# A transformer feed-forward: the last third of its columns computed as a pair of blocks with seven products in place of eight

## The reference, cut to what matters

```
h2 = RMSNorm(x)
g  = silu(dwconv3(h2 @ ffn_w_gate) + b)      # depthwise, 3 taps along the tokens
x  = x + (g * (h2 @ ffn_w_up)) @ ffn_w_down
```

## Time and profile before

| | us |
|---|---|
| median of 3 runs (lowest, highest) | 2778.08 (2777.70, 2778.23) |
| the profiled execution's own time | 2778.77 |
| its span, first to last instruction | 2776.6 |
| PE busy | 2725.8 |
| DVE busy | 1725.9 |
| ACT busy | 1233.1 |
| POOL busy | 194.7 |
| mean granted TensorE clock, share of 2.4 GHz | 0.996 |

### The profile page before, as it was taken

The page is one execution under the profiler, slowest core; times in us unless marked ns, Lnnn a source line. Parts: engine busy times, 40 slices in busy tenths (PEclk is TensorE's granted clock), DMA queues, the critical chain, the costliest instruction groups (busy, mean ns, idle before and its releaser), DMA issues.

```text
span 2776.6 us, 34468 instructions
## 1 busy us (share of the span) xinstructions
PE 2725.8 (98%) x13320; PEld 2389.1 (86%) x13320; DVE 1725.9 (62%) x2752; ACT 1233.1 (44%) x1872; POOL 194.7 (7%) x334
## 2 busy tenths in 40 slices
PE   7999999999999999999999999999999999999998
PEld 5677766788888998889998889889899999999998
DVE  3665655688567877577876687784364544545353
ACT  5344463466535447336446354454233333333231
POOL 0100011200110000110001000000000000000000
PEclk9999999999999999999999999999999999999999
DMA  9866768843563443853444744435644333443333
GB/s 306 296 222 225 254 202 334 277 148 108 198 238 130 159 140 108 298 180 117 152 136 143 283 147 133 154 119 178 257 137 163 130 118 113 139 148 127 112 113 101
DMA packets 139202, 488.89 MB, mean 176 GB/s; under 512 B 24768, under 2 KB 37440, under 8 KB 122400
## 3 DMA queue, kind: packets, MB, share of 16 engines
q1 hardware_dynamic: 111904, 383.83, 40.7%
q0 software_dynamic: 27136, 102.86, 10.3%
HBM read 397.78 MB, written 88.84 MB: 175 GB/s over the span
## 4 chain that ended last, share of the span: by engine, by line
PE 88%; DMA 4%; DVE 3%; ACT 2%; issue 1%; SPq 0%; POOL 0%; DVEq 0%; ACTq 0%; POOLq 0%
PE bank L1488 43%; PE bank L1504 20%; PE bank L1460 10%; PE bank L1474 7%; PE bank L1567 2%; PE bank L1588 2%; PE bank L1577 2%; DMA cat_lo<-cat_scratch 1%; DMA wraw<-w_out_t 1%; PE bank L1533 1%; PE bank L1553 1%; DVE weights L1086 0%; DVE cc L1189 0%; ACT weights L784 0%; DMA wraw<-w_in_t 0%
## 5 line engine op out<-in xcount | busy, mean ns | idle before, releaser
L1488 PE MATMUL bank<-hw_hi,weights 128*128 128x430 f32 (+1 forms) x4224 | 1190.9, 360 | 0.0
L1488 PEld LDWEIGHTS bank<-hw_hi,weights 128*128 128x128 f32 x4224 | 794.9, 188 | 52.9 <-issue 22.4
L1488 PE MATMUL bank<-hw_lo,weights 128*128 128x430 f32 (+1 forms) x2112 | 755.8, 358 | 0.0
L1086 DVE TENSOR_TENSOR weights<-wraw,weights 128x1024 fp32r<-128x1024 f32 x418 | 510.0, 1220 | 207.2 <-ACT weights L784 206.9
L1504 PE MATMUL bank<-mid,weights 128*128 128x428 f32 x3168 | 629.3, 359 | 0.0
L1504 PEld LDWEIGHTS bank<-mid,weights 128*128 128x128 f32 x3168 | 595.7, 189 | 38.2 <-issue 12.2
L784 ACT ACTIVATE weights<-wraw 128x1024 fp32r<-128x1024 f32 x418 | 440.9, 1055 | 418.4 <-DMA wraw<-w_down_t 272.4
L1189 DVE SCALAR_TENSOR_TENSOR cc<-win,par,cc 128x512 f32<-128x512 f32 x600 | 414.1, 746 | 0.0
L1488 PEld LDWEIGHTS bank<-hw_lo,weights 128*128 128x128 f32 x2112 | 398.8, 189 | 16.6 <-issue 1.0
L1460 PE MATMUL bank<-h_hi,weights 128*128 128x512 f32 x1120 | 367.9, 401 | 13.1 <-DVE weights L1086 13.0
L1460 PEld LDWEIGHTS bank<-h_hi,weights 128*128 128x128 f32 x1120 | 212.5, 190 | 83.8 <-issue 37.3
(11 more groups left out here) (144 smaller groups left out, 1963.3 us busy)
## 6 DMA issues: line engine op xcount, KB each, us to landing
wraw<-w_ffn_t SPq DMA_DIRECT2D x264, 512.0 KB, 3.4
weights<-weight_scratch SPq DMA_DIRECT2D x88, 1024.0 KB, 6.2
wraw<-w_down_t SPq DMA_DIRECT2D x132, 512.0 KB, 3.5
weight_scratch<-weights POOLq DMA_DIRECT2D x22, 1024.0 KB, 7.8
hw_raw<-h_scratch SPq DMA_DIRECT2D x24, 430.0 KB, 4.7
yb<-x_scratch SPq DMA_DIRECT2D x48, 214.0 KB, 3.6
y_t<-yb POOLq DMA_DIRECT2D x48, 214.0 KB, 3.0
cat_hi<-cat_scratch SPq DMA_DIRECT2D x10, 1024.0 KB, 8.3
```

Of the source, the lines that this page charges most:

```text
L1086: nc.vector.tensor_tensor(wlo[n % RING], wraw[n % RING][:], whi[n % RING].bitcast(F32), ALU.subtract) \
L1488: mm = nc.tensor.matmul(out, l[:, k, :], r[:, k, 1:TC + 1] if s else r[:, k, :], start=(k == 0 and j == 0), stop=(k == KT - 1 and j == 2))
```

## The change

The six windows become four plain ones of `TC` = 438 columns (`PLAIN` = 4) and one pair of blocks of `TP` = 406 columns (`TQ` = 408 with the taps' margin). The plain ones run as before. The pair comes after all slots, as a list of its own, `PROD`.

Gate or up of two hidden tiles and both blocks is a product of 2 x 2 blocks: A (weights) is 2 hidden tiles by 2 halves of the 1024 channels, B (activations) is 2 halves of the channels by 2 column blocks. Winograd's form of Strassen's algorithm makes it of seven products with 512 channels each, of 12 matmuls: four sums of weight parts (S1 to S4), four sums of window parts (T1 to T4), and results that are added up partly in the banks (product 6 goes onto 1, then 7 and 4 onto it; 3 onto 5) and partly by DVE (`pair_add`), with ACT copying intermediate states of the banks to `e_buf` (`copy_product`). Group 2i is gate and group 2i+1 is up of hidden tiles 2i and 2i+1: 22 groups. T4 and S4 have the sign that lets product 4 be accumulated.

Down is done as before in number of matmuls, in six passes (`PASSES`): one over 2 hidden tiles, five over 4; each part of a pass is 24 matmuls on a weight tile of 128 x 512, and each pass ends in 16 additions to `yb2`. The order on PE is, from the second group on: products 1 and 5 of a group, product 4 of the one before, a down pass if one is due, then 6, 2, 3, 7.

A weight tile is now 128 x 512 (`part_high` on ACT, `part_low` on DVE, three products ahead, `LEAD`; five high buffers, `HI_RING`). The sums S1 to S4 are made by POOL (`part_sum`) for every group but the first, whose sums are made by DVE during the last plain half, as are T1 to T4; five of the seven window parts are split there, two (T3, T4) in the first steps of the pair. The first of the three taps goes from DVE to ACT (`pair_tap0`), with the bias in the swish. SP loads the four parts of a group two groups ahead (A22 up to three), as soon as the product that read the buffer is over; y's residual for both blocks comes in two loads. POOL stores the pair's outputs after all its sums.

```diff
-TC = 428
-WINDOWS = 6
+PLAIN, PAIRS = 4, 1
+TP = 406
+TC = 2 * -(-(TOKENS + 1 - 2 * PAIRS * TP) // (2 * PLAIN))
...
+KH = KT // 2
+ROW_PAIRS = FT // 2
+GROUPS = 2 * ROW_PAIRS
+PASSES = [[0]] + [[i, i + 1] for i in range(1, ROW_PAIRS, 2)]
+A_OF = {1: "A11", 2: "A12", 3: "S4", 4: "A22", 5: "S1", 6: "S2", 7: "S3"}
+B_OF = {1: "B11", 2: "B21", 3: "B22", 4: "T4", 5: "T1", 6: "T2", 7: "T3"}
+SUMS_READ = {"A11": 3, "S1": 2, "S2": 4, "A12": 4, "S4": 4, "S3": 3, "A22": 1}
+HI_RING = 5
+LEAD = 3
...
+            PROD += [("P", _q, _g, 1), ("P", _q, _g, 5)]
+            if _g > 0:
+                PROD.append(("P", _q, _g - 1, 4))
+            if _s == 0 and _i > 0 and PASS_OF[_i] != PASS_OF[_i - 1]:
+                PROD += [("D", _q, PASS_OF[_i - 1], _j) for _j in range(down_parts(PASS_OF[_i - 1]))]
+            PROD += [("P", _q, _g, _p) for _p in (6, 2, 3, 7)]
...
+for _gi in range(ALL_GROUPS):
+    _gate = _gi % 2 == 0
+    for _e, _p in enumerate((1, 5, 6)):
+        ACT_AT[at(_gi, _p) + 1].append(("copy", _gi, _e))
+    for _x, _p in enumerate((2, 3, 7, 4)):
+        _t = at(_gi, _p) + 1
+        if _x < 3:
+            DVE_AT[_t].append(("add", _gi, _x))
+        if _gate:
+            ACT_AT[_t].append(("tap0", _gi, _x))
+        else:
+            DVE_AT[_t].append(("product", _gi, _x))
+            ACT_AT[_t].append(("mid_high", _gi, _x))
...
+    _t = max(_t, _k - (1 if PROD[_k][0] == "D" and PROD[_k][3] >= 3 else LEAD))
...
+        ACT_AT[_t].append(("high", _k))
+        DVE_AT[_t].append(("low", _k))
...
+        if _gate:
+            DVE_AT[_t + 1].append(("taps", _gi, _x))
+            ACT_AT[_t + 2].append(("swish", _gi, _x))
+        elif _x == 3 and _t < PRODS and PROD[_t][0] == "D":
+            DVE_AT[_t].append(("mid_low", _gi, _x))
+        else:
+            DVE_AT[_t + 1].append(("mid_low", _gi, _x))
...
+    DVE_AT[_k + 1].append(("y_add", _k))
...
+    for _a, _k in (("A11", at(_gi - 2, 1)), ("A12", at(_gi - 2, 2)), ("A22", at(max(_gi - 3, 0), 4)), ("A21", at(_gi - 2, 7))):
+        SP_AT[max(_k, at(_gi - 2, 1)) + 1].append(("weights", _gi, _a))
...
+            def part_sum(gi, a):
+                n = 4 * gi
+                if gi >= 2 and a != "S3":
+                    pool.wait_ge(s_used, SLOTS + at(gi - 2, {"S1": 5, "S2": 6, "S4": 3}[a]) + 1)
...
+                two = {"S1": ("A21", "A22"), "S2": ("S1", "A11"), "S3": ("A21", "A11"), "S4": ("A12", "S2")}[a]
...
+                nc.gpsimd.tensor_tensor(p_raw[part_key(gi, a)][:], p_raw[part_key(gi, two[0])][:], p_raw[part_key(gi, two[1])][:],
+                                        ALU.add if a == "S1" else ALU.subtract).then_inc(s2_s, 1)
...
+            def part_low(k):
+                t = PROD[k]
+                dve.wait_ge(s_whi, SPLITS[-1] + k + 1)
+                if t[0] == "P":
+                    gi = GROUPS * t[1] + t[2]
+                    dve.wait_ge(s2_s, 4 * gi + SUMS_READ[A_OF[t[3]]])
+                nc.vector.tensor_tensor(p_lo[part_of(k)][:], p_raw[part_of(k)][:], p_hi[k % HI_RING][:].bitcast(F32),
+                                        ALU.subtract).then_inc(s_wlo, 1)
...
+            def pair_product(k, q, g, p):
+                gi = GROUPS * q + g
+                gate = gi % 2 == 0
+                pe.wait_ge(s_wlo, SPLITS[-1] + k + 1)
...
+                if p == 1 and gi >= 2:
+                    pe.wait_ge(s_c3 if gate else s_m, H_PLAIN + 4 * hidden_pair(gi - 2) + 4)
+                elif p == 5 and gi >= 1:
+                    pe.wait_ge(s2_add, 3 * (gi - 1) + 2)
+                elif p == 2 and gi >= 1:
+                    pe.wait_ge(s2_add, 3 * (gi - 1) + 1)
+                elif p == 6:
+                    pe.wait_ge(s2_e, 3 * gi + 1)
+                elif p == 7:
+                    pe.wait_ge(s2_e, 3 * gi + 3)
+                elif p == 3:
+                    pe.wait_ge(s2_e, 3 * gi + 2)
+                elif p == 4:
+                    pe.wait_ge(s2_add, 3 * gi + 3)
...
+                for t in range(KH):
+                    for j, (l, r) in enumerate(((a, hi), (a, lo), (b, hi))):
+                        mm = nc.tensor.matmul(out, l[:, t, :], r[:, t, cols], start=(p in (1, 2, 5) and t == 0 and j == 0),
+                                              stop=(t == KH - 1 and j == 2), skip_group_check=(p in (3, 4, 6, 7)))
...
+            def pair_down(k, q, F, j):
+                pe.wait_ge(s_wlo, SPLITS[-1] + k + 1)
...
+                for n, o, i in y_outputs(k):
+                    if j == 0:
+                        pe.wait_ge(s_mlo, H_PLAIN + 4 * u + (3 if i == 1 else 4))
+                    if n >= 4:
+                        pe.wait_ge(s_y, Y_PLAIN + n - 3)
```

More of the change, by code:

```diff
@@ L72 @@
 PHASES += [("A", CHUNKS - 1, 0, A_HEAD), ("O", 0), ("A", CHUNKS - 1, A_HEAD, PROJ)]
-for _w in range(WINDOWS):
+for _w in range(PLAIN):
     PHASES.append(("F", _w, 0))
@@ L662, in _ @@
                         load_residual(c)
+                if n in PAIR_LOADS:
+                    load_pair_window(0, PAIR_LOADS[n])
+                if n == LAST + GU_TILES:
+                    for a in ("A21", "A22", "A11", "A12"):
+                        load_part(0, a)
+            for a in ("A21", "A22", "A11", "A12"):
+                load_part(1, a)
+            for d in range(3):
+                load_down(d)
+            for k in range(PRODS):
+                for t in SP_AT[k]:
+                    if t[0] == "weights":
+                        load_part(t[1], t[2])
+                    elif t[0] == "down":
+                        load_down(t[1])
+                    elif t[0] == "window":
+                        load_pair_window(t[1], t[2])
+                    elif t[0] == "y":
+                        load_pair_y(t[1], t[2])
         @block.gpsimd
@@ L1080, in _ @@
                         window_high(0, p)
+                if n in PAIR_ACT:
+                    pair_window_high(*PAIR_ACT[n][1:])
+            for k in range(FIRST_SPLITS):
+                part_high(k)
+            for k in range(PRODS + 4):
+                for t in ACT_AT[k]:
+                    if t[0] == "copy":
+                        copy_product(t[1], t[2])
+                    elif t[0] == "tap0":
+                        pair_tap0(t[1], t[2])
+                    elif t[0] == "swish":
+                        pair_swish(t[1], t[2])
+                    elif t[0] == "mid_high":
+                        pair_mid_high(t[1], t[2])
+                    elif t[0] == "high":
+                        part_high(t[1])
+                    elif t[0] == "window_high":
+                        pair_window_high(t[1], t[2])
         @block.vector
@@ L1331, in y_add, with first_part_sum @@
                                         ALU.add).then_inc(s_y, 1)
+            def first_part_sum(a):
+                two = {"S1": ("A21", "A22"), "S2": ("S1", "A11"), "S3": ("A21", "A11"), "S4": ("A12", "S2")}[a]
+                for t in two:
+                    if t in SUM_ORDER:
+                        dve.wait_ge(s2_s, SUM_ORDER.index(t) + 1)
+                    else:
+                        dve.wait_ge(s2_w[t in ("A21", "A22")][0], 32)
+                nc.vector.tensor_tensor(p_raw[part_key(0, a)][:], p_raw[part_key(0, two[0])][:], p_raw[part_key(0, two[1])][:],
+                                        ALU.add if a == "S1" else ALU.subtract).then_inc(s2_s, 1)
@@ L1375, in _ @@
                     norm2_add(before[1], before[2])
[L1376 removed]
+                if now[0] == "D" and now[2] == 1 and now[1] + 1 < PLAIN and 3 <= now[3] < 3 + PIECES:
                     window_low(now[1] + 1, now[3] - 3)
@@ L1411, in _ @@
                         window_low(0, p)
-                conv_ops(*CONV_OPS_AT[n])
+                if n in PAIR_DVE:
+                    t = PAIR_DVE[n]
+                    if t[0] == "window_sum":
+                        pair_window_sum(*t[1:])
+                    elif t[0] == "window_low":
+                        pair_window_low(*t[1:])
+                    else:
+                        first_part_sum(t[2])
+                conv_ops(*CONV_OPS_AT[n])
+            for k in range(FIRST_SPLITS):
+                part_low(k)
+            for k in range(PRODS + 4):
+                for t in DVE_AT[k]:
+                    if t[0] == "add":
+                        pair_add(t[1], t[2])
+                    elif t[0] == "taps":
+                        pair_taps(t[1], t[2])
+                    elif t[0] == "product":
+                        pair_product(t[1], t[2])
+                    elif t[0] == "mid_low":
+                        pair_mid_low(t[1], t[2])
+                    elif t[0] == "low":
+                        part_low(t[1])
+                    elif t[0] == "y_add":
+                        pair_y_add(t[1])
+                    elif t[0] == "window_sum":
+                        pair_window_sum(t[1], t[2])
+                    elif t[0] == "window_low":
+                        pair_window_low(t[1], t[2])
         @block.tensor
```

377 lines of the change are left out of this document (363 added, 14 removed), and 3 rows, old and new, of the table PAIR_DVE.

## The result

| | before | after |
|---|---|---|
| median, us | 2778.15 (4 runs) | 2813.86 (4 runs, 2811.38 to 2817.82) |
| ratio, 95% interval | | 1.0133 (1.012 to 1.0147) |
| the profiled execution's span | 2776.6 | 2816.0 |
| mean granted clock | 0.996 | 0.988 |

The account below looks back on a forecast made before the run. PE, busy for 98% of the span, was taken to bound the kernel; -51.9 for PE, +7.0 of small terms and +17 of lateness gave -27.9 us on 2778.8, so 2750 us, with 2730 to 2790 as the 8-in-10 range.

Parts of the forecast that it names:

- What PE gains: PE's matmuls: two windows go, the pair and ten more columns in four plain windows come, together -51.9 us.
- The rival of a spacing that stays at 195 ns: Matmuls on PE: weight loads set a floor, so shorter ones save nothing; 2776 us, no change; chance 0.05.
- The turns of ACT and DVE: Pair's product groups: ACT and DVE wait in turn, about 15.7 us against PE's 15.70; lateness +17 us, 0 to 45.
- The sums on GpSimd: 84 sums of 128 x 512 in the pair, taken at 1.2 us each, fit in time and cost nothing by themselves.
- the lateness: Pair's 22 groups: DVE's low parts late by 0.8 us a group, +17 us; forecast of 2750 us, chance 0.43.
- The rival's price for them: Pair: sums exclude DVE's two-SBUF-input instructions, 3.4 us in about 18.5 groups, +63 us, 2796 us; chance 0.26.
- the kernel without lateness: Rival that PE alone binds in the pair, the 17 us gone: 2733 us, 2729 to 2737; chance 0.26.
- (a): Start of the pair: first low part stands behind the last plain y add, PE stands for 1.4 us.
- (b): First two groups: splits of T3 and T4 come between and group 1's tiles load late; 0 to 4 us, 1.5 taken.
- (c): First down pass: each part fills all four banks and the next waits for a y add, 2.0 us.
- (d): Later down passes: each starts behind the x3 chain, 0 to 1 us each, 0.3 taken, 1.5 us in all.
- (e): Tail after the last matmul, 8.8 us: two adds and two stores in place of one, +0.6 us.

Follow-up runs that it names:

- e4: Changed kernel with the 84 sums on DVE instead of POOL and ACT writing the high part first in each step of the pair: 2735.5 us.
- e8: e4 with DVE making the first three low parts before the last plain y add: 2734.1 us, ratio to the kernel before 0.984.
- e1: Changed kernel with GpSimd writing a constant in place of each sum S1 to S4 of 21 groups: 2757.6 us.
- e6: Changed kernel with GpSimd copying one of the two tiles in place of each sum, ACT's order unchanged: 2773.2 us.

## Why the prediction was wrong, point by point

**What PE gains (-51.9 us): right but for one term.** 0.1867 for a product matmul against 0.1869, a pass of 98.06 us in e4 against 98.5. The ten columns more of the plain windows cost 5.4 ns a matmul in down (0.2002 against 0.1948), not 4.0, and the pair began 30 us later instead of 25.3. The rival of a spacing that stays at 195 ns is refuted by the same rows.

**The turns of ACT and DVE: right in mechanism, near in size.** 17 us were put for groups that just reach PE's time; the run without exclusion shows 21 (2757.6 - 2736.5). That the size came so near is in part luck: it was an assumed 5% of error, with 0 and 45 us as ends. The single steps came out at 2.41 and 3.6 us where 2.3 and 3.55 were worked out, with ACT's tap0 at 0.64 rather than 0.54 as the term that was short.

**The sums on GpSimd: the failed step.** The prediction put them at nothing and their exclusion of DVE at a chance of 0.26, as a rival to the lateness. As a term of the forecast they were 0 us; measured are 56 (2813.9 - 2757.6). The rival's price for them, +63, came near, but in part by luck: it had DVE held off for four whole sums of 1.2 us a group, less 1.4 us that DVE's waits would take in, 3.4 in all. In the trace a sum takes 1.6 us in the median, DVE is stretched by 54/21 = 2.6 us a group, and its waits take in nothing. Besides, it was counted from the kernel without lateness, 2733 + 63 = 2796, as if a group that is stretched were not also one whose turns just reach PE's time. Both happen at once; by the prediction's own terms 2733 + 17 + 63 = 2813 (measured 2813.9), by the measured ones 2736.5 + 21 + 56. The prediction itself said that DVE has hardly any slack to give and that the sums fall on the steps that are to make up the lag; from that the two had to be added, and the range to reach to 2813. It ended at 2790, below even the rival's own 2796. The chance was low because no row of the trace before shows POOL computing; absence of a row was read as evidence.

**What the prediction did not see.** It took ACT's order within a step as given and never asked what it is worth. That order is what turns the 5 us that sums on POOL cost into 56.

**The small terms.** (a) 1.4 us at the start: shown, and gone in e8. (b) T3 and T4: 5.8 us in place of 1.5, outside its bounds. The split of one is itself stretched beside a sum, to 2.92 us from 1.85; PE's stop at that place is 2.8 us with constants in place of the sums (e1) and 0.4 in e4. (c) 2.3 against 2.0. (d) 5.9 us in the five later starts against 1.5: 4.6 for low parts of weights, not for the x3 chain, and 1.3 at the last. The first start, which was not in the sum, waits 4.6 us for the low part of `mid`; in e4 it is 0.8 there, and 1.3 at the last. (e) The tail runs from 2806.4 to 2816.0, 9.6 us against 9.4.

**The clock.** Not in the sum: in the changed kernel's pair the granted clock is 0.97, and the same 2904 matmuls keep PE busy for 567.9 us against 541.2 in e4, whose clock is 1.00. The start of one stretch at 1.2 GHz, on PE:

```profile
2399.02 0.42 PE L2155 MATMUL bank<-T_hi,part_hi 128*128 128x406 f32 x1 [2.10 <-DVE e L1780]
...
2401.01 0.54 PE L2155 MATMUL bank<-T_hi,part_lo 128*128 128x406 f32 x1
2401.35 0.54 PE L2155 MATMUL bank<-T_hi,part_hi 128*128 128x406 f32 x1
```

After a stop of 2.10 us matmuls start 0.34 us apart, not 0.187. There are nine such stretches in the pair, each at or just after a stop of 2.1 to 5.8 us; three other stops of 2.1 us have none. The 99 matmuls in them lose some 15 us, worked out from their starts; the rest of the 26.7 us is not clock, but in the main the tail of the last matmul before each of some 50 stops. All of it is inside the 77 us above, not beside them, and how much of the 77 would go with the clock alone no run separates.

## What to carry to other kernels

When one engine must prepare operands ahead for another, issue that work first in each step, in front of anything that waits for a third engine; the lead is worth little if the producer stands in a queue behind a wait (73 us of 2814 here). Before elementwise work goes to GpSimd to relieve DVE, count which of DVE's instructions read two SBUF tensors beside it, and add that to the lateness already there, not in place of it. And two rivals that act on the same chain are to be summed as a case of their own.

## What the runs showed of the hardware that was not expected

- GpSimd against DVE is a matter of reads: with a constant written (525 ns a tile) no DVE instruction of two SBUF inputs leaves its 0.64 or 0.69 us; beside a one-input copy a tap grows to at most 0.99 us, beside a two-input sum to 1.68. The 11 adds with an operand in a bank that ran beside a sum stayed at 0.57 us.
- It works both ways: the 16 copies of e6 that ran beside no two-input DVE instruction took 0.61 to 0.62 us, the longest beside one 1.08. A GpSimd add of 128 x 512 takes 1.27 us at best and 1.61 in the median, 2.7 at most.
- What the exclusion costs is set by the order around it: 54 us of stretched DVE instructions cost 56 us in one order of ACT's list, 72 us of them cost 5 in the other.
- In the changed kernel's pair twelve stops of PE took 2.1 to 5.8 us, and nine of them were followed by a stretch at 1.2 GHz: 0.97 against 1.00 in granted clock, some 15 us more for the same matmuls.
